# Last block of a two-stage transformer kernel: where the conv norm's squares, the last gate tile and the pointwise layer's inputs are computed

## The reference

```python
h = x * (1.0 + scale) + shift
proj = h @ w_in[l]
q, k, v, g_attn, glu_a, glu_b, g_conv = jnp.split(proj, SPLIT_POINTS_2, axis=-1)
y_attn = banded_sink_attention(q, k, v, rel_bias, sinks[l]) * jax.nn.silu(g_attn)
y_conv = conformer_conv(glu_a, glu_b, ...) * jax.nn.silu(g_conv)
y = jnp.concatenate([y_attn, y_conv], axis=-1) @ w_out[l]
x = layer_norm(ALPHA * x + gate * y, ln_g[l], ln_b[l])

def conformer_conv(glu_a, glu_b, conv_w, conv_b, ln_g, ln_b, w_pw, b_pw):
    u = glu_a * jax.nn.sigmoid(glu_b)
    u = causal_depthwise_conv(u, conv_w, width=31) + conv_b
    u = jax.nn.silu(layer_norm(u, ln_g, ln_b))      # over 1024 channels
    return u @ w_pw + b_pw
```

## Time and profile before

| | |
|---|---|
| median of 3 runs | 3430.2 us (3428.87 to 3430.25) |
| the profiled execution's own time | 3426.16 us |
| its span, first to last instruction | 3424.5 us |
| PE busy | 3236.7 us, 95% of the span |
| DVE busy | 2239.1 us, 65% |
| ACT busy | 1325.3 us, 39% |
| mean granted TensorE clock | 0.973 of full speed |

### The profile page before, as it was taken

One profiled execution on the slowest core, in us unless ns is written; L12 is line 12 of the kernel. 1 busy time (PEld: TensorE's weight loads), 2 busy tenths in 40 slices (PEclk: granted clock), 3 DMA queues, 4 the chain that ended last, 5 costly groups with the idle time before them and its releaser, 6 DMA issues.

```text
span 3424.5 us, 48169 instructions
## 1 busy us (share of the span) xinstructions
PE 3236.7 (95%) x16626; PEld 2634.7 (77%) x16626; DVE 2239.1 (65%) x3518; ACT 1325.3 (39%) x2023; POOL 264.5 (8%) x490
## 2 busy tenths in 40 slices
PE   5899999999999999989999999999988998998996
PEld 0799998788777777879788777777876777787785
DVE  0677777756777756676656777765586998454446
ACT  0446545323444443245323444443235221444323
POOL 0000011011111101100101000000110000000000
PEclk7899999999999999999999999999999999999998
DMA  9665556555444425635655444322652222221232
GB/s 398 243 229 203 198 210 220 184 209 201 139 155 156 159 87 182 223 141 206 231 196 184 158 142 154 134 102 102 226 191 111 86 98 86 83 83 55 99 122 86
DMA packets 107405, 554.36 MB, mean 162 GB/s; under 512 B 17856, under 2 KB 17904, under 8 KB 64144
## 3 DMA queue, kind: packets, MB, share of 16 engines
q1 hardware_dynamic: 47232, 343.95, 27.8%
q0 software_dynamic: 60048, 208.75, 17.9%
HBM read 530.55 MB, written 22.04 MB: 161 GB/s over the span
## 4 chain that ended last, share of the span: by engine, by line
PE 74%; DVE 9%; DVEq 6%; DMA 5%; issue 3%; ACT 2%; ACTq 1%; SPq 0%; POOLq 0%; POOL 0%
PE acc L1123 21%; PE acc L1125 21%; PE acc L1124 21%; DVEq L2127 4%; DVE w_lo L1511 3%; PE pv L1245 3%; DMA xy<-in_wm 2%; PE S L1219 2%; DMA gates<-in_wm 1%; PE S L1234 1%; DVE xy L2134 1%; DVE gates L1561 1%; PE pv L1473 1%; PE misc L1256 1%; ACT w_hi L624 1%
## 5 line engine op out<-in xcount | busy, mean ns | idle before, releaser
L1123 PE MATMUL acc<-h_hi,w_hi 128*128 128x512 f32 (+1 forms) x4576 | 1676.6, 366 | 34.5 <-DVE w_lo L1511 19.6
L1125 PE MATMUL acc<-h_hi,w_lo 128*128 128x512 f32 (+1 forms) x4576 | 1644.6, 359 | 0.0
L1124 PE MATMUL acc<-h_lo,w_hi 128*128 128x512 f32 (+1 forms) x4576 | 1643.3, 359 | 0.0
L1123 PEld LDWEIGHTS acc<-h_hi,w_hi 128*128 128x128 f32 x4576 | 867.8, 190 | 193.2 <-issue 48.2
L1124 PEld LDWEIGHTS acc<-h_lo,w_hi 128*128 128x128 f32 x4576 | 868.5, 190 | 129.8 <-issue 7.5
L1125 PEld LDWEIGHTS acc<-h_hi,w_lo 128*128 128x128 f32 x4576 | 867.5, 190 | 129.7
L1511 DVE TENSOR_TENSOR w_lo<-raw,w_hi 128x1024 fp32r<-128x1024 f32 x592 | 697.8, 1220 | 247.6 <-ACT w_hi L624 244.5
L624 ACT ACTIVATE w_hi<-raw 128x1024 fp32r<-128x1024 f32 x592 | 592.7, 1052 | 60.9 <-DMA raw<-in_w 34.5
L624 ACT ACTIVATE ev<-acc 128x512 f32<-128x512 f32 (+1 forms) x210 | 110.5, 530 | 911.0 <-PE acc L1125 889.8
L450 POOL DMA_DIRECT2D gates<-in_wm x288 | 152.9, 531 | 1453.3 <-DVE gates L1561 1260.3
L624 ACT ACTIVATE work<-S,small 128x768 f32<-128x768 f32 (+1 forms) x160 | 129.0, 812 | 256.0 <-DVE small L1673 255.9
(11 more groups left out here) (236 smaller groups left out, 2465.4 us busy)
## 6 DMA issues: line engine op xcount, KB each, us to landing
raw<-in_w SPq DMA_DIRECT2D x296, 1024.0 KB, 4.9
gates<-in_wm POOLq DMA_DIRECT2D x288, 512.0 KB, 4.7
xy<-in_wm SPq DMA_DIRECT2D x32, 1024.0 KB, 8.5
x_d<-xy POOLq DMA_DIRECT2D x2, 4096.0 KB, 13.6
qb<-x_d POOLq DMA_DIRECT2D x16, 256.0 KB, 3.8
kb<-x_d POOLq DMA_DIRECT2D x16, 256.0 KB, 3.9
out_y<-xy POOLq DMA_DIRECT2D x4, 1024.0 KB, 4.1
bias_d<-kb POOLq DMA_DIRECT2D x8, 384.0 KB, 20.7
```

What stands on the lines that cost most here:

```text
L1123: mm(o, w_hi[:, w], h_hi[:, x], start=n == 0, stop=False)
L1124: mm(o, w_hi[:, w], h_lo[:, x], start=False, stop=False)
L1125: last = mm(o, w_lo[:, w], h_hi[:, x], start=False, stop=n == len(ks) - 1)
```

## The change

It has three parts.

1. **Conv norm.** The value tiles' transposes move into the fourth `kv2` tile and the first query tile. The mean's matmul moves from behind the third `kv2` tile into the first query tile. DVE splits that tile's weights before it finishes the taps. The squares go through four buffers (`ev[0]` and three places of `work`), DVE adds them up (`add_squares`), and one matmul against ones, placed before the eleventh k-tile of the first gate tile, replaces eight. `normalise` now runs in steps 1 to 4, two tiles a step.
2. **Last gate tile.** The gate tile of step 7 takes its k-tiles in the order 8 to 15, 0 to 7 (its weights are rolled to match). Behind its fourth k-tile stand step 7's product with the values and step 8's scores.
3. **Pointwise inputs.** They go to `h_hi` and `h_lo` places 8 to 15, which are free when half the last gate tile is done, so that ACT splits three before and five behind the last attention read-out. The free places 0 to 7 take `out2`'s first eight inputs: ACT and DVE split four at the end of each of the two `pw` iterations.

```diff
@@ norm_buffers
-            return t2, t1, misc, (ev[0], ev[2])
+            return t2, t1, misc, [ev[0]] + [work[:, 3072 + SEQ * n:3072 + SEQ * (n + 1)] for n in range(3)]
@@ ACT, attn2
+            def pw_input(k):
+                act.wait_ge(half_done, shown(half_done, j_at("attn2", 7, 1) + 1))
+                f(tile(h_hi, 8 + k, SEQ), tile(xy, 8 + k, SEQ)).then_inc(hhi_done, 1)
...
+                    if not attn and p == 0:
+                        value_columns(1)
+                        act.wait_ge(conv_done, shown(conv_done, CONV0["glu"] + 8))
+                        squares_to_add("cln", SEQ, 0, base=8)
+                        squares_to_add("cln", SEQ, 1, base=8)
+                    if not attn and p == 1:
+                        deviation("cln", SEQ, 8)
...
+                if not proj:
+                    gate_half(i - 1)
+                    for k in range(3, 8):
+                        pw_input(k)
@@ ACT, pw (at the end of an iteration)
+                for s in range(4):
+                    f(tile(h_hi, i * 4 + s, SEQ), tile(xy, i * 4 + s, SEQ)).then_inc(hhi_done, 1)
-            split_y("g", SEQ)
+            split_y("g", SEQ, KT // 2, KT)
@@ PE
-            square_sums("cln", SEQ, 8)
+                def beside_query():
+                    kv2_transposes(1)
+                    mean("cln", SEQ)
+                def beside_gate():
+                    pe.wait_ge(vt_evac, shown(vt_evac, VT0["kv2"] + 2))
+                    added_squares_sum("cln", SEQ)
+                weight_tile(j_at("attn2", 0, 0), a_at("attn2", 0, 0), SEQ, h2, beside=beside_query)
+                weight_tile(j_at("attn2", 0, 1), a_at("attn2", 0, 1), SEQ, h2, beside=beside_gate, beside_n=10)
...
+                def beside_gate():
+                    attn2_values(1, 7)
+                    attn2_scores(1, 8)
+                product(acc[a.odd][:, :], j, [*range(KT // 2, KT), *range(KT // 2)],
+                        beside=beside_gate, beside_n=4).then_inc(tile_done, 1)
+                attn2_transposes(8)
+                attn2_values(1, 8)
@@ DVE
+            def cln_squares():
+                less_mean("cln", SEQ, 8)
+                centre("cln", SEQ, 0, base=8)
+                centre("cln", SEQ, 1, base=8)
+                nc.vector.memset(t1[:], 0.0)
+                add_squares("cln", SEQ, 0)
+                add_squares("cln", SEQ, 1)
+                dve.drain()
+                dve.sem_inc(sqsum_ready, 1)
```

More of the change, by code:

```diff
@@ L886, in squares_to_add @@
                     act.wait_ge(d_ready, shown(d_ready, At(D_AT[c] + n + 1, 4, g)))
[L887 to L899, removed]
+                    f(to[n][:, 0:T], part(c, base + g * 4 + n, T), ACT.Square).then_inc(sq_ready, 1)
             def deviation(c, T, count):
                 _, var, bank, _ = norm_buffers(c)
-                act.wait_ge(sq_used, shown(sq_used, SQ_AT[c] + (1 if c == "c" else count)))
+                act.wait_ge(sq_used, shown(sq_used, SQ_AT[c] + 1))
                 f(var[:, 0:T], bank[:, 0:T], ACT.Ln, scale=1.0 / (count * P), bias=eps[:, 0:1])
@@ L1022, in _ @@
                     act.wait_ge(gs_done, shown(gs_done, 8))
+                if p == 3:
+                    value_columns(0)
                 act.wait_ge(tile_done, shown(tile_done, j + 1))
                 f((k2[:, 0:512], k2[:, 512:1024], ev[3][:], ev[1][:])[p], acc[a.odd][:, :]).then_inc(acc_free, 1)
[L1025 to L1030, removed]
             def conv_silu(i):
@@ L1058, in attn2 @@
                               bias=sink[:, bass.ds(i * 2 + (e - 2), 1)]).then_inc(e2_done, 1)
+                    if not proj and p == 1:
+                        for k in range(3):
+                            pw_input(k)
                     if attn and p == 1:
@@ L1369, in mean @@
                 mm(pv[:, 0:T], ones[:], t1[:, 0:T], start=True, stop=True).then_inc(mean_done, 1)
[L1371 to L1377, removed]
             def added_squares_sum(c, T):
[L1381 to L1382 removed]
+                _, squares, bank, _ = norm_buffers(c)
+                pe.wait_ge(sqsum_ready, shown(sqsum_ready, SQ_AT[c] + 1))
+                mm(bank[:, 0:T], ones[:], squares[:, 0:T], start=True, stop=True).then_inc(sq_used, 1)
             grant(pe, half_done, tile_done, s_ready, t_done, pv_done, vt_done, sq_used, pv2_done)
@@ L1426, in _, with kv2_transposes @@
             loop(pe, 1, 4, glu)
[L1427 to L1431, removed]
+            def kv2_transposes(v):
                 pe.wait_ge(acc_free, shown(acc_free, a_at("kv2", 0, 2 + v) + 1))
@@ L2118, in _, with taps @@
             TAP_PARTS = (range(0, 10), range(10, 20), range(20, TAPS))
-            def taps(c, part):
+            def taps(c, part, between=None):
                 u = tile(xy, c + 8, SEQ)
                 for tap in TAP_PARTS[part]:
+                    if between is not None and tap == 26:
+                        between()
                     w = vec("dw", c * TAPS + tap)
@@ L2212, in attn2 @@
                             last.then_inc(p2_ready, 1)
-                if proj:
-                    dve.wait_ge(acc_free, shown(acc_free, a_at("attn2", i, 1) + 1))
-                    stt(tile(xy, i, SEQ), evt[:], 1.0, ev[3][:], ALU.add, ALU.mult).then_inc(gate_used, 1)
+                if silu:
+                    normalise("cln", SEQ, 6, 2, i)
+                if proj and gate:
+                    gate2(i)
                 if silu:
                     conv_silu(i)
+                if not proj:
+                    for k in range(8):
+                        dve.wait_ge(hhi_done, shown(hhi_done, H_AT["pw"] + k + 1))
+                        tt(tile(h_lo, 8 + k, SEQ), tile(xy, 8 + k, SEQ), tile(h_hi, 8 + k, SEQ).bitcast(F32),
+                           ALU.subtract).then_inc(hlo_done, 1)
+                    gate2(i - 1)
+                    dve.drain()
                 if attn:
```

196 lines of the change are left out of this document (102 added, 94 removed).

## The result

| | before | after |
|---|---|---|
| median, 4 runs each on one chip | 3429.53 us (3427.23 to 3430.25) | 3389.41 us (3387.55 to 3390.75) |
| profiled execution: its time, its span | 3426.16, 3424.5 us | 3388.58, 3386.8 us |
| mean granted TensorE clock | 0.973 | 0.978 |

The account below looks back on a forecast made before the run. PE, at 95% of the span, bounds the kernel; its idle places and low clock were to give 19.6 + 12.6 + 5.5 = 37.7 us, taken as 37. From 3426.16 plus 4.0 for the median: 3393 us, range 3388 to 3401.

Parts of the forecast that it names:

- The sum: Whole change: gains of 19.6 at the conv norm, 12.6 at the last gate tile and 5.5 at out2, 37.7 us.
- the step from the profiled execution to the median: Whole kernel: median of the runs taken as 4.0 us above the profiled execution, from 3389.2 to 3393.2 us.
- the adds with a drain: Conv norm on DVE: each addition of squares with the drain in front of it costs 0.77 us.
- the fp32 matmul: Conv norm on PE: each fp32 matmul against ones costs at most 0.97 us, taken as 0.85.
- the cover of 1.9 us: First gate tile: sum of squares ready 1.9 us before PE reaches it at the eleventh k-tile; counted as no wait.
- The remaining wait: Behind the last gate tile: PE waits 1.0 us for the attention read-outs before step 8's product with the values.
- Rival A: New waits at the square sum, the second head and `h_lo` eat a part: gain 29, 3401 us; chance 0.11.
- B: Low clock stays behind the small gaps left in the three places: gain 30, 3400 us; chance 0.09.
- C: Clock falls in PE's dense part, 2887 to 3425: five tiles at low clock give 3439 us; chance 0.02.
- D: Steps 1 to 4: the engines that feed PE become the bound, about 3428 us, no change; chance 0.03.
- idle time of 2 us or more: Old trace's conv norm, last scores and out2: every low clock stretch was said to follow such a gap.
- part 2's clock term: Behind the last gate tile, 3164 to 3209: the low clock after the idle time goes, a gain of 1.8 us.

Follow-up runs that it names:

- the weave alone: Changed kernel with step 7's values and step 8's scores behind the last gate tile, early pointwise input splits kept: 3400.09 us, ratio 0.9915 to before.
- part 3 undone: Changed kernel with all sixteen out2 inputs split after pw, as before the change: 3393.73 us, ratio 0.9901 to before.
- part 1 by itself: Changed kernel with the last gate tile, pointwise inputs and out2 splits taken back, only the conv norm's change kept: 3405.57 us, ratio 0.9935 to before.

## Why the prediction was right

Forecast 3393 us, measured 3389.4. The sum, 37.7 us, is also the difference of the two spans, 3424.5 less 3386.8; that this comes out so exactly is luck, since both last blocks happen to start within 0.15 us of each other where the starts spread over 5.4. By the pieces it is 37.55. The 3.8 us between 3393.2 and the median are 0.6 of the gain (37.6 between the profiled executions, where I took 37) and 3.2 of the step from the profiled execution to the median: I took 4.0 us, as before, and it was 0.8 this time. It follows no mechanism: the profiled execution of before, 3426.16 us, was a quick one among runs of 3424.71 to 3430.25. Such a step is better kept in the range.

- **Part 1**, 19.6 us predicted, 19.91 measured. Each step held: the adds with a drain at 0.78 to 0.79 (0.77 predicted), the fp32 matmul at 0.86, and the cover of 1.9 us, which the two kernels with an earlier sum measure from outside. The eight additions never took 1.1 us, so the flush that VectorE: DVE Perf Modes of the Trainium skill describes in "The DRAIN you can't avoid" isn't seen in their pace. The same section adds that a next operation that is not held starts earlier, which the prediction had left out.
- **Part 2**, 12.6 predicted (10.8 up to `pw`, 1.8 behind it for the clock), 12.13 measured (10.57 and 1.56). Of the 10.57, 8.9 are waits (9.91 less 1.05); the rest is mostly the transposes, slow behind the waits in the kernel before (3.4 us against 1.7). The prediction's sum had this in it and didn't name it. The remaining wait is 1.05, predicted 1.0. Taken back, the weave alone costs 10.84.
- **Part 3**, 5.5 predicted, 5.84 less 0.32 measured. Waits of 0.64 and 0.51 us stand where 0.8 and 0.5 were worked out.
- **Rival A** is false: the only new waits are those two. **B** is false for the change: the wait of 1.05 us stands in seven of the traces, and those of some 0.65 and 0.5 us in nine, each time at a clock of 1.00 over the next 5 us. As a mechanism it is true: with the scores four k-tiles later the clock falls. **C** is false: steps 1 to 7 have 188.0 us in thirteen of fourteen traces. **D** is false in the changed kernel; the fourteenth, with `normalise` in step 0, waits 1.33 us there, which is as near as it comes.

One step was right with a wrong reason. I gave the low clock in `pw` and `out2` as a follower of "idle time of 2 us or more". That is how the old trace's last block reads, but it is no rule, and the old trace itself says so. Ahead of the last block, PE has a wait of 3.13 us near 2378 us and one of 2.46 us near 2606 us, the same to 0.01 us in all fourteen traces. By the table of stretches for the 5 us behind each, the first is followed by a clock of 0.50 in six of them, of 0.66 to 0.68 in five and of 1.00 in three; the second by 1.00 in ten and by 0.66 or 0.67 in four. (The clock has two levels, 1.00 and 0.50; a value between them is a stretch with both.) The wait of 3.13 us before and with part 3 undone:

```profile
2376.69:2381.69 5.00, 5.00 (x12) 3.61 (x12) 5.00 (x9) 4.27 (x9) 0.00 (x0) 0.50 0.05 20
```

```profile
2377.91:2382.91 5.00, 5.00 (x20) 3.81 (x21) 5.00 (x9) 4.28 (x9) 0.00 (x0) 1.00 0.06 23
```

And the wait of 2.46 us before and after:

```profile
2605.63:2610.63 5.00, 5.00 (x22) 4.16 (x23) 0.06 (x1) 5.00 (x8) 0.00 (x0) 1.00 0.16 66
```

```profile
2605.87:2610.87 5.00, 5.00 (x15) 4.00 (x16) 0.06 (x1) 5.00 (x8) 0.00 (x0) 0.66 0.15 59
```

PE has 22 matmuls in these last 5 us before and 15 after. So the full clock behind the 2.91 us of the earlier sum is one outcome and not a limit. And the same wait of 3.74 us at `out2` had unequal sequels, by the table of stretches for the 5 us behind it: before, with part 3 undone, and with part 1 by itself.

```profile
3212.00:3217.00 5.00, 4.26 (x10) 3.42 (x11) 5.00 (x9) 5.00 (x11) 0.91 (x2) 0.50 0.33 105
```

```profile
3179.00:3184.00 5.00, 4.21 (x10) 3.38 (x11) 5.00 (x9) 5.00 (x11) 0.97 (x2) 0.50 0.31 105
```

```profile
3189.00:3194.00 5.00, 4.60 (x13) 3.67 (x14) 5.00 (x10) 5.00 (x10) 0.57 (x2) 0.66 0.33 108
```

The piece to the first `out2` read-out was 17.66, 17.34 and 16.47 us for them, and the rest of that piece is the same work in all three. Which of two equal gaps is followed by a longer stretch at 1.2 GHz stays open; a gap should be priced with a range. Here that is 0.2 us on top of the wait of 2.91 (3.15 less 2.91) to 2.7 on top of the wait of 3.74 (17.66 less 3.74, and less the 11.2 us that the piece has in after without its own 0.64). That part 2's clock term came out near its 1.8 us (1.56) is therefore luck in part: with part 1 by itself nearly the same waits ahead of `pw` left `pw` at full clock.

## What to carry to other kernels

Where the busiest engine is at 95%, read its timeline for the brackets and take, piece by piece, what each place costs beyond its matmuls; fill each with work that already exists on the same engine, placed just behind what makes it ready. Work out the cover of every new wait, then measure it by moving the consumer earlier: two such runs gave 1.9 us twice. Don't take one trace for what the clock does behind a wait. And compare pieces between common events, since the spans of single runs carry some us from elsewhere.

## What the runs showed that I had not expected

Small waits can cost more than their length: 1.9 us of new waits between light transposes cost 3.9 us, of which 1.6 are the product with the values at the low clock (4.46 us instead of 2.82), while 0.74 us of new waits cost 0.91. The other surprise is the last block's start, which moved over 5.4 us between traces without any edit before it; equal waits with unequal sequels, as the two above, are one source of that, and whether there are others stays open.
